# A two-layer decoder trunk: weights split ahead of use, division by the norm moved behind the product, and an output projection in two halves

## The reference, cut to what matters

```
for l in 0, 1:
    h = rms_norm(x, g0);  z = h @ w_in[l]          # 1024 x 1024
    y_main = pool_mixer(z_main) if l == 0 else dilated_mixer(z_main, positions, shared)
    y = concat(y_main, memory_attn(z_mem, mem)) @ w_out[l]
    x = x + rms_norm(y, g1)
    h = rms_norm(x, g2)
    y = (silu(h @ w_gate) * (h @ w_up)) @ w_down   # inner width 2816
    x = x + rms_norm(y, g3)
    if l == 0: shared = rope(k), v of rms_norm(x) @ w_kv
```

## Time and profile before

| What | us |
|---|---|
| median of three runs | 2314.24 (2311.76 to 2314.56) |
| the profiled execution, its own time | 2309.91 |
| its span, first to last instruction | 2308.0 |
| PE busy | 2150.7 (93%) |
| DVE busy | 1337.2 (58%) |
| ACT busy | 880.6 (38%) |
| POOL busy | 264.9 (11%) |

### The profile page before, as it was taken

How to read it: one execution, slowest core, us unless ns; L and a number is a source line. 1 busy time by engine, 2 the same in 40 slices (tenths; PEclk the granted TensorE clock), 3 DMA queues, 4 the chain that set the end, 5 groups by cost and what they waited for, 6 DMA issues and landing times.

```text
span 2308.0 us, 24943 instructions
## 1 busy us (share of the span) xinstructions
PE 2150.7 (93%) x9554; PEld 1719.2 (74%) x9554; DVE 1337.2 (58%) x1984; ACT 880.6 (38%) x1375; POOL 264.9 (11%) x136
## 2 busy tenths in 40 slices
PE   5997999999999999987999999895999999999996
PEld 4775877888888887875777767673788888888785
DVE  7355287566666626456445446469846666662543
ACT  5335343222223425232545556564422222242420
POOL 4442100000000000043122215120000000000000
PEclk9998999999999999998999999997999999999998
DMA  4202051222223536450000000014222222262533
GB/s 155 89 14 94 25 177 50 82 83 82 82 82 120 200 129 211 129 203 18 19 28 28 28 25 12 24 47 146 83 78 82 82 82 82 101 222 90 208 122 107
DMA packets 69382, 214.77 MB, mean 93 GB/s; under 512 B 7825, under 2 KB 10129, under 8 KB 64017
## 3 DMA queue, kind: packets, MB, share of 16 engines
q1 hardware_dynamic: 53136, 183.82, 23.1%
q10 hardware_dynamic: 16128, 29.37, 3.8%
HBM read 170.04 MB, written 43.12 MB: 92 GB/s over the span
## 4 chain that ended last, share of the span: by engine, by line
PE 79%; DVE 12%; issue 3%; ACT 3%; DMA 2%; POOL 0%; ACTq 0%; SPq 0%; DVEq 0%
PE PS L772 10%; PE PS L773 10%; PE PS L774 10%; PE PS L589 8%; PE PS L590 7%; PE PS L592 7%; PE PS L792 7%; PE PS L794 6%; PE PS L793 6%; PE PSC L697 4%; PE PO L671 2%; DVE SS L1436 2%; DVE RSTD L1428 1%; PE PTR L681 1%; DVE PR L1539 1%
## 5 line engine op out<-in xcount | busy, mean ns | idle before, releaser
L792 PE MATMUL PS<-IH,DH 128*128 128x512 f32 x704 | 275.7, 392 | 3.3 <-DVE IL L1744 2.9
L794 PE MATMUL PS<-IH,DL 128*128 128x512 f32 x704 | 274.0, 389 | 0.0
L793 PE MATMUL PS<-IL,DH 128*128 128x512 f32 x704 | 274.0, 389 | 0.0
L772 PE MATMUL PS<-BHT,SH 128*128 128x512 f32 x576 | 224.1, 389 | 0.0
L773 PE MATMUL PS<-BLT,SH 128*128 128x512 f32 x576 | 224.1, 389 | 0.0
L774 PE MATMUL PS<-BHT,SL 128*128 128x512 f32 x576 | 224.1, 389 | 0.0
L589 PE MATMUL PS<-XH,WH 128*128 128x512 f32 x448 | 196.0, 437 | 26.7 <-DVE XL L1566 21.2
L590 PE MATMUL PS<-XL,WH 128*128 128x512 f32 x448 | 180.7, 403 | 0.0
L2073 POOL TENSOR_TENSOR WR<-WR,GN 128x1024 f32<-128x1024 f32 x28 | 59.8, 2140 | 1003.8 <-DMA WR<-in_w 983.6
L2079 POOL TENSOR_TENSOR WL<-WR,WH 128x1024 fp32r<-128x1024 f32 (+2 forms) x66 | 145.3, 2203 | 217.0 <-ACT WH L899 217.0
L772 PE MATMUL PS<-BH,SH 128*128 128x512 f32 x432 | 168.0, 389 | 0.0
(11 more groups left out here) (205 smaller groups left out, 4327.8 us busy)
## 6 DMA issues: line engine op xcount, KB each, us to landing
DR<-in_wdn SPq DMA_DIRECT2D x64, 704.0 KB, 4.1
SR<-in_wst SPq DMA_DIRECT2D x36, 1024.0 KB, 5.2
WR<-in_w SPq DMA_DIRECT2D x60, 512.0 KB, 3.5
IR<-inner SPq DMA_DIRECT2D x88, 256.0 KB, 5.7
inner<-TP SPq DMA_DIRECT2D x36, 512.0 KB, 4.4
TP<-x_mid ACTq DMA_DIRECT2D x48, 256.0 KB, 3.0
x_mid<-YOA ACTq DMA_DIRECT2D x32, 256.0 KB, 2.7
XS<-in_x SPq DMA_DIRECT2D x16, 256.0 KB, 6.3
```

The lines of the kernel that those rows point to most:

```text
L772: MM(BANK[bank], SH[b][:, w, c], BH[t][:, k, :], start=(k == 0), stop=False)
L792: MM(bank, wh[:, i, :], IH[r][:, :], start=(k == 0), stop=False)
L793: MM(bank, wh[:, i, :], IL[r][:, :], start=False, stop=False)
L794: ins = MM(bank, wl[:, i, :], IH[r][:, :], start=False, stop=(k == NF - 1))
```

## The change

It has these parts.

1. **Weights split early.** The 24 weight tiles of layer 1's `mem`, `in` and `kv` jobs are prepared during the first 16 pairs of layer 0, one in even pairs and two in odd ones (`prepared`). SP loads a tile, ACT multiplies its eight blocks with the gain and makes the high part, POOL subtracts, and SP stores both parts in DRAM (`w_keep`). When the job comes, both parts are loaded (1 MB where it was 512 KB), and ACT and POOL have nothing to do for it.
2. **Norms in columns.** PE multiplies the sum of squares with a single column (four products of one column each), ACT takes the root of 128x4, DVE inverts 128x4, and PE transposes the four columns, widened to 128, to rows, which ACT copies (`norm_columns`, `norm_rows`). The two parts stand two to four blocks apart in PE's list.
3. **Unnormalised operand in layer 1's ffn.** The residual times the gain is split at once, and the norm's factor is multiplied in behind the products: for the ffn jobs in `gate_scaled` and `product`, for the pairs in `scale_pair`. `st_add` and the multiplication of y with the norm's factor go to POOL in layer 1.
4. **Divided output projection.** `out` of layer 1 is done in two halves of four blocks, each by halves of columns. The first memory tile's attention comes first, the second one's last; 91 steps stand in the stage jobs (the first of the second stage has none), 40 in the 16 jobs of the first half of `out`. The weights have 16 slots of their own, loaded in their turn.
5. **Banks.** The `mem` jobs take the attention's banks, `out` in layer 1 and its ffn go round over four (the last eight over seven).
6. **Start.** x is split in tiles of 128x1024, the squares come later, POOL waits for the split, DVE splits weights 6 and 7. `x_low` of the first half comes behind the last sum of layer 0.

The diff, cut:

```diff
-            run += [Job("out", 1, m, kn=5, tag="early") for m in range(KT)]
...
+            for part in range(2):
+                jobs += [Job("out", 1, m, k0=4 * part, kn=4, halves=(h,), tag=(part, h), slot=10 + 8 * part + m,
+                             share=("out", 1, m, (part, 0)) if h else None) for h in range(2) for m in range(KT)]
...
+def presplit(o):
+
+    return o.l == 1 and o.name in ("mem", "in", "kv")
...
+def prepared(f):
+
+    a, b = (len(PRE) * min(max(g - NHT, 0), PRE_PAIRS) // PRE_PAIRS for g in (f, f + 1))
+    return range(a, b)
...
-        counts = [7] * 6 + [5, 6, 6] + [5, 5, 6] * 3
+        counts = [5, 5, 6, 0] + [5, 5, 6] * 4 + [5, 6]
...
+            HOOKS[J[("out", 1, m, (0, 0))]] = (1, 2, 3) if m < 5 else (1, 3)
+            HOOKS[J[("out", 1, m, (0, 1))]] = (0, 1, 2, 3) if m < 2 else (1, 3) if m < 7 else (1,)
```

PE's new norm, with `PRE_PAIRS` = 16 and `NV` = 3 buffers for the weights' preparation:

```diff
+            def norm_columns(s, h):
...
+                for t in range(4):
+                    c = HT * h + P * t
+                    ins = MM(PX[:, t:t + 1], SS[:, c:c + P], ONE, start=True, stop=True)
...
+            def norm_rows(s, h):
...
+                    ins = nc.tensor.transpose(PX[:, P * t:P * (t + 1)],
+                                              RC[:, 4 * h + t:4 * h + t + 1].to_broadcast([P, P]), IDENT)
```

ACT's preparation of a weight, and where it stands in the pairs:

```diff
+            def keep_weight(i):
...
+                act.wait_ge(v_loaded[b], 16 * (i // NV + 1))
+                for k in range(KT):
+                    ins = A(VR[b][:, k, :], VR[b][:, k, :], ACT.Copy, scale=GN[:, 8 * o.gain + k:8 * o.gain + k + 1])
+                    ins.then_inc(v_gained, 1)
+                act.wait_ge(v_gained, KT * (i + 1))
+                A(VH[b][:, :, :], VR[b][:, :, :], ACT.Copy).then_inc(v_hi, 1)
...
                     p1_copy(q)
-                    silu_first(q)
+                    if l == 0:
+                        silu_first(q)
+                        for i in prepared(f):
+                            keep_weight(i)
                     if f < NF - 1:
                         st_raw_hi(q + 1)
                         st_sum_hi(q + 1)
```

ACT in layer 1's ffn, DVE's `scale_pair`, and POOL's added work (the subtraction for the kept weights, then layer 1):

```diff
                     gate(l, 3, 0)
+                    for k in range(KT):
+                        scale_x(0, k)
                     norm_root(s_x, 1)
...
+            def scale_pair(q):
...
+                V.tensor_tensor(G[:, :], G[:, :], RSTD[:, :], ALU.mult).then_inc(g_scaled, 1)
...
+                link(V.tensor_tensor(UP[:, :], UP[:, :], RSTD[:, :], ALU.mult))
...
+            for i in range(len(PRE)):
+                pool.wait_ge(v_hi, i + 1)
+                G_.tensor_tensor(VL[i % NV][:, :, :], VR[i % NV][:, :, :], as_f32(VH[i % NV][:, :, :]),
+                                 ALU.subtract).then_inc(v_lo, 1)
...
+            y_norm(0)
+            y_norm(1)
+            for q in range(NPAIR, 2 * NPAIR):
+                st_add(q)
```

SP in the pairs (its `keep_weight` stores both parts, once they are there):

```diff
                     load_pair(l, f)
                     keep_pair(l, f - 2)
+                    if l == 0:
+                        for i in prepared(f - 2):
+                            keep_weight(i)
+                        for i in prepared(f):
+                            load_kept(i)
```

More of the change, by code:

```diff
@@ L44 @@
 XDEPTH = 3
+MEM_IN, POS_IN, MASK_IN = 16, 32, 48
 NLOAD = 10
@@ L187, in banks @@
         return ((o.i // 2) % 4,)
-    return tuple(2 * (n % 2) + h for h in ((0,) if o.name == "mem" else o.halves))
+    if o.name == "mem":
+        return (4 + o.i % 3,)
+    if o.name == "out" and o.l == 1:
+        part, h = o.tag
+        return ((4, 5, 6, 0, 1, 2, 3, 4)[o.i] if part and h else o.i % 4 if part else o.i % 4,)
+    if o.name == "ffn" and o.l == 1:
+        return ((2 * o.i[0] + o.i[1]) % 4,)
+    return tuple(2 * (n % 2) + h for h in o.halves)
 PRODUCT_READ = ("p1_done", "u2_done", "c11_done", "u3_done", "v2_done", "c21_done", "c12_done")
@@ L1820, in sub_layer @@
-                    residuals(r, 0, (6, 7))
-                    for n in range(4):
-                        weight_lo(ffn[n])
-                    norm(s_y, 1)
-                    norm(s_x, 0)
-                    normed(r, 0, range(KT))
+                    for m in range(KT):
+                        add_y(m, 0)
+                        accumulate(s_y, 0, m - 1 if m else 0)
+                    accumulate(s_y, 0, KT - 1)
+                    add_y(0, 1)
+                    invert(s_y, 0)
+                    add_y(1, 1)
@@ L1826, in sub_layer @@
+                    for k in range(KT):
+                        accumulate(s_x, 0, k)
+                    add_y(5, 1)
+                    invert(s_x, 0)
+                    weight_lo(ffn[3])
+                    gate_scaled(0, 0)
+                    product(l, 0, 0)
+                    add_y(6, 1)
+                    add_y(7, 1)
+                    for k in range(KT):
+                        accumulate(s_y, 1, k)
+                    gate_scaled(1, 0)
                     weight_lo(ffn[4])
+                    product(l, 1, 0)
@@ L2033, in _ @@
                     group_max(0)
[L2034 to L2045 removed]
+                if n == 6:
+                    split_low(6, 15)
+            for h in range(2):
+                for m in range(KT):
+                    for _ in HOOKS[J[("out", 1, m, (0, h))]]:
                         step()
[L2047 to L2049 removed]
+                    if h and m >= 2:
+                        combine_last(m - 2)
             sub_layer(1)
[L2051 removed]
+            invert(7, 1)
             for k in range(KT):
@@ L2279, in _ @@
             loads_to(J[("out", 0, 0, 0)])
-            for h in range(2):
-                sp.wait_ge(x_lo[h], 8)
+            sp.wait_ge(x0_lo, KT)
             sub_layer(0)
```

913 lines of the change are left out of this document (552 added, 361 removed).

## The result

The changed kernel took **2402.64 us** (median of four runs, 2399.94 to 2410.70) and the kernel before 2313.89 beside it: ratio **1.0391**, 95% interval 1.0365 to 1.0417. It is slower by 89 us, where 2304 was forecast. The profiled execution has a span of 2400.3 us, against 2308.0.

A forecast was written before the change was run, and what follows sets the result against it. PE was taken to bound the pairs, with gains only in other stages, where PE waits or runs at lower clock. 2309.9 - 7 - 9 - 4 - 3 - 24 - 25 + 62 = 2299.9, so 2304 as median; range 2262 to 2335.

The forecast's parts named there:

- Layer 0's pairs: Layer 0's 18 pairs: preparing weights there stalls PE 1.4 and 4.8 us in alternation; 62 us lost with the clock.
- w: Layer 0's pairs: time each prepared weight puts ahead of the next pair's high parts on ACT, 3.4 us (2.7 to 3.8).
- each stall of 4.8 costs 1.5 more: Layer 0's pairs with two weights: lower PE clock after the stall, 12 us in all.
- rival A: Layer 0's pairs: every stall lowers the clock and w is 3.8; 83 us lost, total 2325; chance 0.22.
- `down`: Two `down` stages: the inversion ahead of splits that PE needs goes, 2 us each, 4 gained.
- The boundary: Between the layers: POOL's work vanishes, DVE's low parts and sums shorten, two inversions less; 24 us gained, perhaps 16.
- Layer 1 up to its pairs: Layer 1's attention, `out` and head of ffn: 70 us lost before, 45 after; 25 gained (0 to 40).
- 13 + 12 + 4 + 16: Layer 1 before its pairs, losses in the new order: stages 13, `out` jobs 12, hand-over 4, ffn 16; 45 us.
- Rival B: Front of layer 1 gives nothing back, new waits fill the old ones' place; total 2329; chance 0.12.
- Start: Start and pooling: first norm complete at 45 us, pooling starts near 58 instead of 65.7; 7 us gained (0 to 14).
- layer 0's `out` and ffn: Layer 0's `out` and ffn: of 24 us lost, 9 taken back from waits around norms and their half-clock stretch.
- the tail: Last 21.80 us: the norm's chain, which stands bare there, shortens; 3 us gained.

The follow-up runs named there:

- run 4: Changed kernel, with a semaphore each for the loads of inner tiles 20 and 21 (two tables' semaphores merged): 2392.24 us.
- Run 5: Changed kernel with the edits of run 3 and run 4, plus the boundary norm's four products ahead of the first `mem` job: 2308.59 us.
- run 9: Changed kernel with the edits of run 3, run 4 and Run 5, plus later memory values and earlier stores of memory tiles: 2308.50 us.
- run 8: Changed kernel with the edits of run 3 and run 4, plus reordered squares, sums and additions in layer 1's ffn: 2309.69 us.
- run 10: Changed kernel with edits of run 3, run 4, Run 5, run 7, run 8, run 9, plus last two ffn weights split early: 2288.34 us, 0.9882 of kernel before.
- run 7: Changed kernel with the edits of run 3 and run 4, plus scores alternating between two banks in 16 `out` jobs of layer 1: 2315.28 us.
- run 12: run 10's kernel without the combination of the second group of dilated heads in `out`: 2277.99 us.
- run 3: Changed kernel with ACT's order altered in layer 0's pairs: first weight prepared before the first silu, second behind the next high parts: 2325.54 us.
- Run 6: Changed kernel with the edits of run 3 and run 4, plus y's multiplication by its norm back on DVE: 2317.09 us.

## Why the prediction was wrong

**Layer 0's pairs, +77.7 and not +62: mechanism and stalls right, clock mis-sized.** Forecast: stalls of 1.4 and 4.8 us in turn and w = 3.4. Measured: 1.50, 4.95 and 3.44. DVE's low part was held for 0.95 (2.70 against 1.75 in the earlier trace rows), forecast 0.8. The term that failed is "each stall of 4.8 costs 1.5 more": it came from one row, 3.42 us at 0.57. Here 5.71 us ran at 0.50, and two pairs take 47.8 us, which is 38.1 + 1.5 + 4.95 + **3.3**. Eight times 9.7 are the 77.7. The trace of before had dearer cases, such as this one behind a wait of 7.06 us:

```profile
1065.74:1071.20 5.46, 5.46 (x13) 3.84 (x13) 2.87 (x3) 0.00 (x0) 0.00 (x0) 0.50 0.00 0
```

In sum this is rival A's clock, 3.0, with the forecast's w, but not A's mechanism: A put half of it behind each stall, and all of it came behind the long one. (The rows without a gain in the earlier trace rows are squares and not copies; w came out right even so.)

**`down`: a part of the change I priced at nothing.** I wrote -4 and did not ask what the halved number of semaphores makes late. The second and third job of each layer's `down` lost 10.6 us together; run 4 took back 8.5, and the other 2.1 stay open. The norm itself behaved: the two jobs at the middle of `down` lose 1.7 us and not 3.0 each. The rest is the end of layer 0's second half: 1.3 more for the norm at its 13th job, and 3.0 us of waiting for the memory's reload, where it had been 0.3.

**The boundary: -12.8, not -24.** The norm stood 12.5 us from its last sum to its copy, where I took "two inversions less"; the memory values cost a wait of 4.7, and reloads of x three waits of 1.5 to 2.5. Run 5 shows the first to be worth 2 to 6.6; run 9 shows that the others replace each other.

**Layer 1 up to its pairs: +19.5, not -25, and this is the step that failed most.** I counted 45 us of new losses, 13 + 12 + 4 + 16. For the ffn I counted 16; it lost 39 over PE's need (126.2 - 87.2). Runs 8 and 10 took back 18 of them by order alone, without less work. I had named the late sums and POOL's slowing of DVE, but costed each by itself and not what queued behind each wait.

For stages and `out` I came out 21 too low, and all of it lies in `out`. The stages' products, steps, 13 us and most of the 15 for transposes and norms come to some 350 us at my prices, and they took 350.2. `out` needs 87 us for products and 50 for its steps; it took 178.4, so 41 are lost, where I had 12 + 4. The hand-over took 8.9 us and 3.0 more at half clock behind it. The first of its jobs took 16.9 us, some 10 more than products and steps: PE waited 4.85 us for a copy that stood behind ACT's four rearranging copies of a key and query tile,

```profile
1486.85 4.13 ACT L1478 ACTIVATE TP<-PS 32x1024 f32<-32x1024 f32 x4
```

then 2.55 us for DVE, and ran at half clock. No run touched this. The other 18 or so lie in the steps between the short products: one bank is 4 to 5 of them (run 7) and the combination 7, with 6 more of its 13 at the hand-over (run 12). The rest stays open. Rival B, that this front gives nothing back, was the nearest, and at 0.12 it was too small; even it was not bad enough.

The stages also say how little came of freeing POOL there. Of the kernel before, the stages without `out`:

```profile
1065.74:1449.22 383.48, 360.62 (x1687) 270.34 (x1687) 199.45 (x563) 207.84 (x452) 100.06 (x43) 0.97 0.07 23
```

It held 107 steps (by the hooks in the code), so (383.5 - 196.1 us of products) / 107 = 1.75 us each. After, (350.2 - 196.1) / 91 = 1.69. POOL fell from 100 to 30 us busy and a step got 0.06 us cheaper, half of it only because the 16 steps that left are of the dear kind with 256 keys. New work on ACT came between the steps as well, and no run frees POOL alone. I had put half of the losses in the stages down to POOL; the trace of before did not bear that out, since the steps I had priced myself (1.65) lay beside 4.2 us of POOL in 16 to 22 us.

**Start: +2.4, not -7.** Pooling began at 63.2, not 58. The first norm's sum was there at 44.6, near the 45 of the forecast, but PE's wait of 7.05 us for it had a price that I left out, the clock behind it:

```profile
44.56:53.75 9.19, 8.61 (x38) 8.15 (x38) 4.63 (x5) 1.57 (x4) 2.52 (x1) 0.50 0.18 57
```

At full clock these 9.2 us would be some 4.6, nearly all that was missing. And the attention there begins when ACT has copied the memory values, at 71.0, no sooner than in the kernel before: ahead of that copy stood a high part whose weight was issued at 61.6 and landed at 70.0. Run 9 did not free it.

**As forecast:** layer 0's `out` and ffn (-7.0 for -9), the tail (-2.4 for -3), layer 1's pairs at 19.04 (their 2.9 are half clock behind a wait of 3.0 ahead of the first), no inversion of 3.35 us.

## What to carry to other kernels

Work that fills idle time of an engine is free only at the place in its queue where the idle time lies: the same 24 preparations cost 78 us in front of a needed operation and 1 us on both sides of it. Price a wait with the clock behind it, and price every wait that a change merges (two transfers on one semaphore make the first as late as the last). When a change moves work off an engine that was not the bound, expect little, and look for what its new order makes late.

## What the runs showed of the hardware

The same instructions get a different granted clock from run to run. The stages of layer 1 are the same code in runs 3, 6 and 7, yet they took 350.2, 359.9 and 356.5 us. Run 6's row, against 350.17 at 0.98 in run 3:

```profile
1048.00:1407.86 359.86, 339.02 (x1561) 257.45 (x1559) 163.25 (x492) 170.60 (x377) 29.00 (x13) 0.95 0.13 44
```

In all, 34 us of this stretch were granted the 1.2 GHz level, against 13.6 in run 3. At the boundary, in the same code, a wait of 2.73 us was followed by no fall at all (run 8), one of 2.74 by 6.8 us at half clock (run 7) and one of 3.02 by 10.2 (the changed kernel). A stage with many waits near 1 to 5 us thus varies by up to 10 us with the work unchanged, and an edit worth less can't be read from the total of one such run.

The norm's four products of one column show as eight records and take PE 0.79 us at full clock and 1.70 at half; a norm in the middle of a job costs PE 1.4 us in all, where the full-width product had cost 0.9 (a `down` job of 8.38 us instead of 7.48). I had counted only that the answer comes sooner. (In the middle of `down` the new form still gains: 1.7 us lost in the two jobs there and not 3.0, since DVE has no inversion.)
